# Seven half-block products for the feed-forward up projection of a three-pass fp32 kernel, with weight sums made on VectorE

## The chip, the cores and the metric

The kernel runs on one core of a Trainium2 chip. The metric is the device time of one execution in microseconds (us), as the median over runs. TensorE (PE) multiplies, VectorE (DVE), ScalarE (ACT) and GpSimd (POOL) work on tiles of 128 partitions, and SyncE (SP) issues the loads.

## The reference, cut to what matters

Two blocks of a network run over 512 tokens of width 1024: an attention and a retention layer with memory attention, then a Hyena and gated-linear-attention block. The change touches only the feed-forward part at the very end:

```python
h2 = _rms_norm(x, norm_mlp[l]) * (1.0 + sc2) + sh2          # 512 x 1024
x = x + g2 * (jnp.square(jax.nn.relu(h2 @ w1)) @ w2)         # w1: 1024 x 4096 ("up"), w2: 4096 x 1024 ("down")
return _rms_norm(x, norm_final)
```

## The kernel before

Activations lie transposed: features on the partitions, 512 tokens along the free axis, in tiles of 128 features. A product in fp32 accuracy is made of three passes in the type fp32r. Each operand is split into a high part, rounded by ScalarE, and a low part, the rest; TensorE adds high by high, high by low and low by high into one bank of PSUM.

Weights come in blocks of 512 x 256, stored as 128 x 1024 (four k tiles of 256 columns). One list, PLAN, orders them, and every engine walks it with its own Feed. take() hands out tile u and first makes the splits of all tiles up to u+2. So the split of tile u+2 stands in an engine's instruction stream at the place where that engine takes tile u. For one tile ScalarE copies raw to wh (high), once TensorE has finished tile u-3 (three buffers, NW); GpSimd subtracts to get wl (low). VectorE does that subtraction only for tiles 0 to 72 and tile 164 (DVE_LOW). raw has five buffers, loaded by SyncE as they come free.

In the feed-forward part an up unit is 256 hidden features: two tiles (k halves), each 24 matmuls of 128x512. The unit's features go to banks 0 and 1. ScalarE takes the ReLU out of the bank into a temporary (T1 or T2 in turn), VectorE squares it, ScalarE makes FHI from it and GpSimd FLO; every third FLO is VectorE's. Group g is four up units, 1024 hidden features; a down step (g, n) multiplies the group by the weights for output columns 256n to 256n+255 in two tiles, and VectorE adds the banks, times the gate, onto X. The order is up(0), up(1), down(0), up(2), down(1), up(3), down(2), down(3). All engines execute in program order, so an instruction that waits holds back what is queued behind it.

The rest of the kernel (the two blocks ahead of the feed-forward part) is laid out by the same Feed and isn't touched.

Of the kernel before, what the change touches and what calls it, by code (L numbers as in the profile page):

```python
# [8 lines left out]
ALU = mybir.AluOpType  # L9
# [29 lines left out]

def weight_plan():  # L40
# [3 lines left out]
    def pair(w, k0, k1, cols):  # L44
        for k in range(k0, k1, 4):
            plan.append(("w", w, k, cols))
# [53 lines left out]
    def up(g):  # L100
        for n in range(4):
            pair("up", 0, 8, (1024 * g + 256 * n,))

    def down(g):
        for n in range(4):
            pair("down", 8 * g, 8 * g + 8, (256 * n,))

    up(0)
    for g in range(1, 4):
        up(g)  # L110
        down(g - 1)
    down(3)
# [3 lines left out]
PLAN = weight_plan()  # L116

# [132 lines left out]
def build(nc, a, out, stack):  # L250
# [126 lines left out]
    E = [at("E%d" % j, [128, T], 142 + 2 * j) for j in range(2)]  # L377
    FHI = [at("FHI%d" % g, [128, 8, T], 92 + 32 * g, F32R) for g in range(2)]
    FLO = [at("FLO%d" % g, [128, 8, T], 108 + 32 * g, F32R) for g in range(2)]
# [5 lines left out]
    def P(name, i=0, n=1):  # L385
        o = PAR[name][0] + i
        return par[:, o:o + n]

# [34 lines left out]
    def tensor(pe):  # L423
# [653 lines left out]
        unit_f(("up", 0, 0), (0, 1), *hi_lo("x3"), hooks=[nothing, first_scale, nothing, nothing])  # L1077

        def up(g):
            for n in range(4):  # L1080
                u = 4 * g + n
                if u:
                    unit_f(("up", g, n), (2, 3) if u == 1 else (0, 1), *hi_lo("x4"), by_k=2 if u == 1 else 0)

        def down(g):
            for n in range(4):
                for kh in range(2):
                    u = feed.take()
                    pe.wait_ge(*(done("l", "f", g, k) for k in range(4 * kh, 4 * kh + 4)))
                    features(("down", g, n), FHI[g % 2], FLO[g % 2], range(4 * kh, 4 * kh + 4), kh == 0, kh == 1, (0, 1), u,  # L1090
                             kh=kh)

        up(0)
        for g in range(1, 4):
            up(g)
            down(g - 1)
        down(3)
# [25 lines left out]
    def vector(dve):  # L1123
# [763 lines left out]
        def norm_half(ks, kh):  # L1887

            def low(k):
                dve.wait_ge(done("h", "x4", k))  # L1890
                stt(HL[:, k, :], bank[4 + k % 2], mod[:, 24 + k:25 + k], HH[:, k, :].bitcast(F32), ALU.add,
                    ALU.subtract).then_inc(*by_dve("l", "x4", k))

            for k in ks:
                dve.wait_ge(done("scale rows", "x3"), done("l", "x4", k - 2) if k > 1 else None, *(done("half", ("up", 0, 0), kh, j) for j in range(2)))
                stt(bank[4 + k % 2], X[:, k, :], gx2[:, k:k + 1], bank[7], ALU.mult, ALU.mult).then_inc(*by_dve("x4", k))
                if k > ks[0]:
                    low(k - 1)
            low(ks[-1])

        norm_half(range(0, 4), 0)
        for j in range(2):
            dve.wait_ge(done("unit", ("up", 0, 0), j), done("scale", "x3"))
            tt(E[j][:, :], bank[j], R[:, :], ALU.mult).then_inc(*by_dve("kept", ("up", 0, 0), j))
# [13 lines left out]
        def up(g):  # L1918
            for n in range(4):
                u = 4 * g + n  # L1920
                if u:
                    feed.unit()
                    for j in range(2):
                        k = 2 * n + j
                        t = turn("hidden", g, k)
                        square(g, k, t)
                        if made[0] % 3 == 0:
                            temp_used("hidden", g, k)
                if u == 1:
                    for j in range(2):  # L1930
                        square(g, j, E[j])

        def down(g):
            for n in range(4):
                feed.unit()
                for j in range(2):
                    t = 2 * n + j
                    dve.wait_ge(done("unit", ("down", g, n), j))
                    if g == 3 and t == 7:
                        for h in range(2):  # L1940
                            c = slice(256 * h, 256 * h + 256)
                            stt(X[:, t, c], bank[j][:, c], mod[:, 40 + t:41 + t], X[:, t, c], ALU.mult, ALU.add).then_inc(*by_dve("last tile", h))
                        by_dve.also("kept", ("down", g, n), j)
                        turn("last", "x5")
                        continue
                    stt(X[:, t, :], bank[j], mod[:, 40 + t:41 + t], X[:, t, :], ALU.mult, ALU.add).then_inc(*by_dve("kept", ("down", g, n), j))
                    if g == 3:
                        add_square("x5", t, T, t == 0, t == 6, free=done("sum", "x3"))

        up(0)  # L1950
        for g in range(1, 4):
            up(g)
            down(g - 1)
        down(3)
# [9 lines left out]
    def scalar(act):  # L1964
# [517 lines left out]
        for j in range(2):  # L2482
            act.wait_ge(done("kept", ("up", 0, 0), j), done("shift kept"))
# [7 lines left out]
        def up(g):  # L2491
            for n in range(4):
                u = 4 * g + n
                if u:
                    feed.unit()
                    for j in range(2):
                        k = 2 * n + j
                        t = temp("hidden", g, k)
                        act.wait_ge(done("unit", ("up", g, n), j), temp_free("hidden", g, k))
                        fn(t[:, :], bank[j + 2 * (u == 1)], ACT.Relu).then_inc(*by_act("relu", g, k))  # L2500
                        by_act.also("kept", ("up", g, n), j)
                        high(g, k, t)
                if u == 1:
                    for j in range(2):
                        high(g, j, E[j])

        def down(g):
            for n in range(4):
                feed.unit()
                for j in range(2):  # L2510
                    t, m = 2 * n + j, done("kept", ("down", g, n), j)
                    if g == 3 and t == 7:
                        q = temp("last", "x5")
                        act.wait_ge(temp_free("last", "x5"))
                        for h in range(2):
                            c = slice(256 * h, 256 * h + 256)
                            act.wait_ge(done("last tile", h))
                            fn(q[:, c], X[:, t, c], ACT.Square).then_inc(*by_act("last square half", h))
                    elif g == 3:
                        square("x5", t, X[:, t, :], T, m)  # L2520
                    if g == 3:
                        act.wait_ge(m, done("unit", ("up", 3, 3), 1))
                        fn(XG[:, t, :], X[:, t, :], ACT.Copy, scale=P("gfin", t)).then_inc(*by_act("weighted", t))

        up(0)
        for g in range(1, 4):
            up(g)
            down(g - 1)
        fn(sm[:, 0:1], one, ACT.Sqrt).then_inc(*by_act())
        down(3)  # L2530
# [10 lines left out]
    def gpsimd(pool):  # L2541
        tt = pool.eng.tensor_tensor

        def split(i, u):
            if u not in DVE_LOW:
# [8 lines left out]
                by_pool.also("raw free", i)  # L2554

# [125 lines left out]
        def low(g, k, t):  # L2681
            made[0] += 1
            if made[0] % 3:
# [4 lines left out]
        def up(g):  # L2688
            for n in range(4):
                u = 4 * g + n  # L2690
                if u:
                    feed.unit()
                    for j in range(2):
                        k = 2 * n + j
                        if low(g, k, temp("hidden", g, k)):
                            by_pool.also("temp", turns["hidden", g, k])
                if u == 1:
                    for j in range(2):
                        low(g, j, E[j])

        up(0)
        for g in range(1, 4):
            up(g)
            units(4)
        units(4)
# [190 lines left out]
def layout(x):  # L2896
# [37 lines left out]
    for i, (kind, w, k, cols) in enumerate(plan):  # L2934
        if kind == "w":
# [40 lines left out]
```

## Time and profile before

| | before |
|---|---|
| median of 3 runs | 1625.59 us (1625.49 to 1627.17) |
| the profiled execution | 1626.04 us, of which the span of the trace is 1624.3 us |
| granted TensorE clock, mean | 0.999 |
| busy: TensorE / VectorE / ScalarE / GpSimd | 99% / 51% / 42% / 36% |

The profiled execution lies 0.45 us above the median, and 1.7 us of it lie outside the span. The page gives busy times by engine, the span in 40 slices, and the chain of work that ended last; the trace behind it gives each instruction with its start, its duration, and what ended the idle time before it. The feed-forward part begins with the first up unit at 1265 us.

### The profile page before, as it was taken

What the parts mean: (1) busy time and instruction counts of PE and PEld (TensorE: products, weight loads), DVE (VectorE), ACT (ScalarE), POOL (GpSimd) and SP (SyncE); (2) the same over time, 40 slices, a digit from 0 to 9 for tenths busy, and PEclk for the clock granted to TensorE, in tenths of its full rate; (3) what the DMA queues carried; (4) which work ended last, traced back from release to release, by engine and by line L of the source; (5) the groups of instructions that cost most, each with busy time, mean ns of one, the idle gap of its engine ahead of it and who ended that gap; (6) DMA issues with size and microseconds to landing.
All of it is one profiled execution on the core that took longest, in us unless ns stands there. A gap on an engine that the chain in (4) does not pass through costs nothing.

```text
span 1624.3 us, 20270 instructions
## 1 busy us (share of the span) xinstructions
PE 1607.9 (99%) x8308; PEld 1336.6 (82%) x8308; DVE 829.1 (51%) x1239; ACT 680.8 (42%) x1043; POOL 583.0 (36%) x289
## 2 busy tenths in 40 slices
PE   9999999999999999999999999999999999999998
PEld 6888898889888878888887767789878788888887
DVE  7787867676665364443443646681356621111112
ACT  6533343443432433555455463423435643332323
POOL 1002113221344434334333434353323465555542
PEclk9999999999999999999999999999999999999999
DMA  6453333343355223233223241122112133222221
GB/s 234 153 204 131 125 127 134 116 132 121 133 205 207 104 91 104 93 103 103 94 90 121 78 156 66 52 87 73 53 40 78 65 117 104 91 103 92 98 85 52
DMA packets 53252, 179.16 MB, mean 110 GB/s; under 512 B 6428, under 2 KB 7068, under 8 KB 52776
## 3 DMA queue, kind: packets, MB, share of 16 engines
q1 hardware_dynamic: 53160, 177.88, 31.5%
q8 instruction: 65, 1.06, 0.3%
q14 instruction: 27, 0.22, 0.0%
HBM read 172.58 MB, written 2.12 MB: 108 GB/s over the span
## 4 chain that ended last, share of the span: by engine, by line
PE 92%; DVE 5%; ACT 1%; issue 1%; DMA 0%; SPq 0%; POOL 0%; DVEq 0%; ACTq 0%; POOLq 0%
PE banks L427 90%; PE banks L430 2%; DVE ACC L1182 1%; DVE wl L1146 1%; ACT T L1969 0%; DMA maskf<-cst_dram 0%; DVE ada L1130 0%; DVE X L1130 0%; ACT wh L1972 0%; ACT Sc L1969 0%; DVE ML L1130 0%; DVE T L1912 0%; ACT L1969 0%; DVE Sc L1130 0%; DVE E L1912 0%
## 5 line engine op out<-in xcount | busy, mean ns | idle before, releaser
L2553 POOL TENSOR_TENSOR wl<-raw,wh 128x1024 fp32r<-128x1024 f32 x171 | 424.2, 2485 | 525.3 <-ACT wh L1972 525.3
L427 PE MATMUL banks<-HH,wh 128*128 128x512 f32 (+1 forms) x1040 | 413.2, 397 | 2.6 <-ACT T L1969 0.9
L427 PE MATMUL banks<-HL,wh 128*128 128x512 f32 (+1 forms) x1040 | 402.3, 390 | 0.3 <-DVE HL L1130 0.3
L1972 ACT ACTIVATE wh<-raw 128x1024 fp32r<-128x1024 f32 x246 | 257.0, 1052 | 296.9 <-PE banks L427 289.0
L427 PE MATMUL banks<-HH,wl 128*128 128x512 f32 x1032 | 282.6, 390 | 0.0
L427 PEld LDWEIGHTS banks<-HH,wh 128*128 128x128 f32 (+1 forms) x1040 | 194.9, 187 | 50.0 <-issue 5.5
L427 PEld LDWEIGHTS banks<-HL,wh 128*128 128x128 f32 (+1 forms) x1040 | 194.7, 187 | 42.0 <-issue 1.4
L427 PEld LDWEIGHTS banks<-HH,wl 128*128 128x128 f32 x1032 | 193.4, 188 | 41.5 <-issue 1.0
L427 PE MATMUL banks<-wh,HH 128*128 128x256 f32 x448 | 128.5, 287 | 0.0
L427 PE MATMUL banks<-wl,HH 128*128 128x256 f32 x448 | 126.7, 283 | 0.0
L427 PE MATMUL banks<-wh,HL 128*128 128x256 f32 x448 | 126.6, 283 | 0.0
L1146 DVE TENSOR_TENSOR wl<-raw,wh 128x1024 fp32r<-128x1024 f32 x74 | 89.5, 1231 | 28.3 <-ACT wh L1972 28.3
L427 PE MATMUL banks<-OH,wh 128*128 128x512 f32 x256 | 103.1, 403 | 0.3 <-issue 0.3
L1130 DVE SCALAR_TENSOR_TENSOR X<-banks,mod,X 128x512 f32<-128x512 f32 (+1 forms) x41 | 30.1, 736 | 142.3 <-PE banks L427 142.3
L427 PE MATMUL banks<-OL,wh 128*128 128x512 f32 x256 | 99.8, 390 | 0.0
L427 PE MATMUL banks<-FHI,wh 128*128 128x512 f32 x256 | 99.6, 389 | 0.0
L427 PE MATMUL banks<-FLO,wh 128*128 128x512 f32 x256 | 99.6, 389 | 0.0
L2562 POOL TENSOR_TENSOR OL<-T,OH 128x512 fp32r<-128x512 f32 x21 | 28.3, 1349 | 197.4 <-ACT OH L1972 197.4
L1912 DVE TENSOR_TENSOR T<-T 128x512 f32<-128x512 f32 x30 | 28.3, 942 | 113.9 <-ACT T L1969 113.8
L427 PEld LDWEIGHTS banks<-wh,HL 128*128 128x128 f32 x448 | 85.7, 191 | 0.5 <-issue 0.2
L427 PEld LDWEIGHTS banks<-wh,HH 128*128 128x128 f32 x448 | 85.7, 191 | 0.5 <-issue 0.2
L427 PEld LDWEIGHTS banks<-wl,HH 128*128 128x128 f32 x448 | 85.7, 191 | 0.0
(354 smaller groups left out, 2627.5 us busy)
## 6 DMA issues: line engine op xcount, KB each, us to landing
raw<-wst_dram SPq DMA_DIRECT2D x294, 512.0 KB, 3.2
X<-xT_dram SPq DMA_DIRECT2D x8, 512.0 KB, 6.6
CB<-sums_dram SPq DMA_DIRECT2D x12, 256.0 KB, 3.1
D<-dec_dram SPq DMA_DIRECT2D x12, 256.0 KB, 2.8
out_dram<-XT SPq DMA_DIRECT2D x8, 256.0 KB
QS<-QX SPq DMA_DIRECT2D x24, 64.0 KB, 2.6
KSw<-KX SPq DMA_DIRECT2D x24, 64.0 KB, 2.0
MX<-memT_dram SPq DMA_DIRECT2D x2, 512.0 KB, 8.7
```

What stands on the lines that cost most here:

```text
L427: return pe.eng.matmul(dst, w, x, start=start, stop=stop, skip_group_check=True)
L430: return pe.eng.transpose(dst, x, ident[:, :])
L1130: return eng.scalar_tensor_tensor(out=dst, in0=x, scalar=s, in1=y, op0=op0, op1=op1)
L1146: tt(wl[:, q, :], raw[:, i % NRAW, :], wh[:, q, :].bitcast(F32), ALU.subtract).then_inc(*by_dve("low", u))
L1182: i = tt(acc[:, 0:n], acc[:, 0:n], q[:, 0:n], ALU.add)
L1912: tt(t[:, :], t[:, :], t[:, :], ALU.mult).then_inc(*by_dve("f", g, k))
L1972: return eng.activation(dst, src, ACT.Copy)
L2553: tt(wl[:, q, :], raw[:, i % NRAW, :], wh[:, q, :].bitcast(F32), ALU.subtract).then_inc(*by_pool("low", u))
L2562: tt(OL[:, tile, :], t[:, :], OH[:, tile, :].bitcast(F32), ALU.subtract).then_inc(*by_pool("l", "o", l, tile))
```

## The change

Up units 4 to 15 are computed by Winograd's form of Strassen's scheme. A tile of 512 x 256 weights and the matching 512 x 512 of activations are cut into 2 x 2 half blocks (two k tiles by 128 output features; two k tiles by 256 tokens). Seven products replace eight; four of them take sums of weight blocks, four take sums of activation blocks. The products of one unit go to halves of banks 2 to 5 and are put together by VectorE. Moving operands become 256 wide. For each such tile (kind "s") ScalarE copies the raw tile to banks 6 and 7, VectorE makes four sums from that copy and the raw tile, ScalarE and GpSimd make their high and low parts. VectorE also makes wl of these tiles. The group becomes two up units (512 hidden features), a down step becomes one tile, and the order becomes: up(0), up(1), then for g from 1 to 7 and h in 0, 1: up(2g+h), down(g-1, 2h), down(g-1, 2h+1); at the end down(7, 0..3). Nothing changes ahead of the second up unit.

```diff
+FF = [("up", 0), ("up", 1)]
+for _g in range(1, 8):
+    for _h in range(2):
+        FF += [("up", 2 * _g + _h), ("down", _g - 1, 2 * _h), ("down", _g - 1, 2 * _h + 1)]
+FF += [("down", 7, _n) for _n in range(4)]
+SEVEN = 4
+NS = 3
# TensorE
+        def seven(u):
+            for kh in range(2):
+                w = feed.take()
...
+                def product(b, c, a, x):
+                    o, s0 = bank[b][:, 256 * c:256 * c + 256], kh == 0 and c == 0
+                    for q in range(2):
+                        mm(o, a[0][:, q, :], x[0][:, q, :], s0 and q == 0, False)
+                        mm(o, a[0][:, q, :], x[1][:, q, :], False, False)
+                    for q in range(2):
+                        i = mm(o, a[1][:, q, :], x[0][:, q, :], False, kh == 1 and q == 1)
+                    return i
+                pe.wait_ge(done("high", w), done("low", w), done("x sums", kh), *free[2])
+                product(2, 0, of_w(1, 0), of_x(1, 0))
+                product(2, 1, of_w(0, 0), of_x(0, 0)).then_inc(*by_pe("seven", u, kh, 0))
+                pe.wait_ge(done("sums high", w), done("sums low", w), *free[3])
+                product(3, 0, of_w(1, 1), of_t(3))
+                product(3, 1, of_s(2), of_t(1)).then_inc(*by_pe("seven", u, kh, 1))
+                pe.wait_ge(*free[4])
+                product(4, 0, of_s(1), of_t(0))
+                product(4, 1, of_s(0), of_t(2)).then_inc(*by_pe("seven", u, kh, 2))
+                pe.wait_ge(*free[5])
+                product(5, 0, of_s(3), of_x(1, 1)).then_inc(*by_pe("seven", u, kh, 3))
...
+        def down(g, n):
+            u = feed.take()
+            pe.wait_ge(*(done("l", "f", g, k) for k in range(4)))
+            features(("down", g, n), FHI[g % 2], FLO[g % 2], range(4), True, True, (0, 1), u)
# VectorE
         def split(i, u):
-            if u in DVE_LOW:
+            if PLAN[i][0] == "s":
...
+                dve.wait_ge(done("copied", u), done("sums low", S_TILES[v - 2]) if v > 1 else done("l", "f", 0, 1))
+                tt(s[:, 0:2, :, :], c[:, 0, :, :, :].rearrange("p q i c -> p i q c"), w[:, :, :, 1, :],
+                   ALU.subtract).then_inc(*by_dve())
+                dve.wait_ge(by_dve.last())
+                tt(s[:, 2, :, :], c[:, 1, :, 1, :], s[:, 0, :, :], ALU.add).then_inc(*by_dve())
+                dve.wait_ge(by_dve.last())
+                tt(s[:, 3, :, :], c[:, 1, :, 0, :], s[:, 2, :, :], ALU.subtract).then_inc(*by_dve("summed", i))
+                dve.wait_ge(done("high", u))
+                tt(wl[:, q, :], psum[:, 6:8, :].rearrange("p b c -> p (b c)"), wh[:, q, :].bitcast(F32),
+                   ALU.subtract).then_inc(*by_dve("low", u))
+                by_dve.also("raw free", i)
+            elif u in DVE_LOW:
...
+        def x_sums(kh):
+            x = XW[:, 4 * kh:4 * kh + 4, :].rearrange("p (j q) (h c) -> p j q h c", q=2, c=256)
...
+            tt(XS[0][:, 0, :, :], b12, b11, ALU.subtract).then_inc(*by_dve())
+            stt(XS[1][:, 0, :, :], b22, -1.0, b12, ALU.mult, ALU.subtract).then_inc(*by_dve())
+            dve.wait_ge(by_dve.last())
+            tt(XS[0][:, 1, :, :], b22, XS[0][:, 0, :, :], ALU.add).then_inc(*by_dve("x summed", kh, 0))
+            dve.wait_ge(by_dve.last())
+            tt(XS[1][:, 1, :, :], b21, XS[0][:, 1, :, :], ALU.subtract).then_inc(*by_dve("x summed", kh, 1))
+        def x_sums_low(kh):
+            for n in range(2):
+                dve.wait_ge(done("x sums high", kh, n), done("x summed", kh, 1))
+                tt(XSL[:, kh, 2 * n:2 * n + 2, :, :], XS[n][:, :, :, :], XSH[:, kh, 2 * n:2 * n + 2, :, :].bitcast(F32),
+                   ALU.subtract).then_inc(*by_dve("x sums", kh))
+        def seven(u):
+            g, n = u // 2, 2 * (u % 2)
+            kept = done("kept", ("up", u - 1), 0) if u > SEVEN else None
+            dve.wait_ge(done("seven", u, 1, 1), done("first product", u), kept)
+            tt(PS[:, 1, :], bank[3][:, 256:512], PS[:, 0, :], ALU.add).then_inc(*by_dve())
+            dve.wait_ge(done("seven", u, 1, 2), by_dve.last())
+            tt(PS[:, 2:4, :], psum[:, 4, :].rearrange("p (a c) -> p a c", a=2), PS[:, 1:2, :].to_broadcast([128, 2, 256]),
+               ALU.add).then_inc(*by_dve())
+            t = turn("hidden", g, n + 1)
+            dve.wait_ge(by_dve.last(), temp_free("hidden", g, n + 1))
+            tt(t[:, :].rearrange("p (a c) -> p a c", a=2), psum[:, 3:5, 0:256], PS[:, 3:4, :].to_broadcast([128, 2, 256]),
+               ALU.add).then_inc(*by_dve("kept", ("up", u), 1))
+            hidden(g, n + 1, t)
+            t = turn("hidden", g, n)
+            dve.wait_ge(done("seven", u, 1, 3), temp_free("hidden", g, n))
+            tt(t[:, :].rearrange("p (a c) -> p a c", a=2), psum[:, 2:6:3, 0:256], PS[:, 0:3:2, :],
+               ALU.add).then_inc(*by_dve("kept", ("up", u), 0))
+            hidden(g, n, t)
+        def hidden(g, k, t):
+            dve.wait_ge(by_dve.last())
+            stt(t[:, :], t[:, :], 0.0, t[:, :], ALU.max, ALU.mult).then_inc(*by_dve("f", g, k))
...
+        def down(g, n):
+            feed.take()
+            for j in range(2):
...
+                stt(X[:, t, :], bank[j], mod[:, 40 + t:41 + t], X[:, t, :], ALU.mult, ALU.add).then_inc(*by_dve("kept", ("down", g, n), j))
...
+            if (g, n) == (0, 0):
+                x_sums_low(0)
+            if (g, n) == (0, 1):
+                x_sums(1)
# in VectorE's up(u): after u == 2 x_sums(0), after u == 3 x_sums_low(1)
# ScalarE
         def split(i, u):
+            if PLAN[i][0] == "s":
+                v = S_AT[u]
+                act.wait_ge(done("low", S_TILES[v - 1]) if v else done("l", "x4", 7))
+                copy(psum[:, 6:8, :].rearrange("p b c -> p (b c)"), raw[:, i % NRAW, :]).then_inc(*by_act("copied", u))
             copy(wh[:, u % NW, :], raw[:, i % NRAW, :]).then_inc(*by_act("high", u))
+            if PLAN[i][0] == "s":
+                act.wait_ge(done("summed", i), done("w free", S_TILES[v - NS]) if v >= NS else None)
+                copy(SH_[:, v % NS, :], WS[:, v % 2, :]).then_inc(*by_act("sums high", u))
...
+            if u >= SEVEN:
+                act.wait_ge(done("seven", u, 1, 0), done("kept", ("up", u - 1), 0) if u > SEVEN else done("x sums", 1))
+                copy(PS[:, 0, :], bank[2][:, 256:512]).then_inc(*by_act("first product", u))
+                for k in (2 * (u % 2) + 1, 2 * (u % 2)):
+                    high(g, k, temp("hidden", g, k))
+                return
# GpSimd
+            if PLAN[i][0] == "s":
+                v = S_AT[u]
+                pool.wait_ge(done("sums high", u))
+                tt(SL_[:, v % NS, :], WS[:, v % 2, :], SH_[:, v % NS, :].bitcast(F32), ALU.subtract).then_inc(*by_pool("sums low", u))
...
+        def x_whole(k):
+            pool.wait_ge(done("h", "x4", k), done("l", "x4", k))
+            tt(XW[:, k, :], HH[:, k, :].bitcast(F32), HL[:, k, :].bitcast(F32), ALU.add).then_inc(*by_pool("x whole", k))
+        def up(u):
+            feed.unit()
...
+            if u in (1, 2):
+                for k in range(4 * u - 4, 4 * u):
+                    x_whole(k)
```

## Rows read from the trace of the kernel before

**Rows 1.** The page: busy time by engine, then the chain that ended last.
```profile
PE 1607.9 (99%) x8308; PEld 1336.6 (82%) x8308; DVE 829.1 (51%) x1239; ACT 680.8 (42%) x1043; POOL 583.0 (36%) x289
PE 92%; DVE 5%; ACT 1%; issue 1%; DMA 0%; SPq 0%; POOL 0%; DVEq 0%; ACTq 0%; POOLq 0%
```
**Rows 2.** Busy time in a stretch: us, PE, PEld, DVE, ACT, POOL (instructions), clock, DMA.
```profile
1439.30:1482.00 42.70, 42.70 (x190) 35.36 (x189) 6.64 (x9) 9.60 (x10) 20.13 (x9) 1.00 0.26 95
```
**Rows 3.** Timeline of TensorE, 512 wide: start, duration, operation, count.
```profile
1402.83 0.39 PE L427 MATMUL banks<-HL,wh 128*128 128x512 f32 x1
1403.05 1.07 PE L427 MATMUL banks<-HH,wl 128*128 128x512 f32 x4
1403.96 0.39 PE L427 MATMUL banks<-HH,wh 128*128 128x512 f32 x1
```
**Rows 4.** Timeline of TensorE, weights from wh and wl, 256 wide.
```profile
31.73 0.28 PE L427 MATMUL banks<-ML,wh 128*128 128x256 f32 x1
32.57 0.64 PE L427 MATMUL banks<-MH,wl 128*128 128x256 f32 x4
33.05 0.28 PE L427 MATMUL banks<-MH,wh 128*128 128x256 f32 x1
```
**Rows 5.** Timeline across engines, a down step and the split beside it.
```profile
1461.34 1.06 ACT L1972 ACTIVATE wh<-raw 128x1024 fp32r<-128x1024 f32 x1 [4.38 <-PE banks L427]
1466.78 1.06 ACT L1972 ACTIVATE wh<-raw 128x1024 fp32r<-128x1024 f32 x1 [4.38 <-PE banks L427]
1450.40 0.75 DVE L1130 SCALAR_TENSOR_TENSOR X<-banks,mod,X 128x512 f32<-128x512 f32 x1 [1.97 <-PE banks L427]
```
**Rows 6.** Groups by form, VectorE: count, busy us, mean ns.
```profile
L1904 DVE TENSOR_TENSOR E<-banks,R 128x512 f32<-128x512 f32 x2 | 1.3, 680 | 0.0
L1368 DVE TENSOR_TENSOR PL<-banks,PH 128x256 fp32r<-128x256 f32 x12 | 5.0, 413 | 0.0
L1130 DVE SCALAR_TENSOR_TENSOR T<-X,gfx,R 128x512 f32<-128x512 f32 x8 | 5.9, 751 | 0.2
```
**Rows 7.** One line of VectorE: duration ns min/median/max.
```profile
L1146 DVE TENSOR_TENSOR wl<-raw,wh x74: 1208/1217/1714, 6.3 to 1074.2; 128x1024 fp32r<-128x1024 f32 x74
```
**Rows 8.** Groups by form, ScalarE and GpSimd.
```profile
L1972 ACT ACTIVATE FHI<-T 128x512 fp32r<-128x512 f32 x30 | 19.0, 633 | 30.3 <-DVE T L1912 30.3
L1969 ACT ACTIVATE banks<-R 128x512 f32<-128x512 f32 x1 | 0.6, 602 | 0.0
L2553 POOL TENSOR_TENSOR wl<-raw,wh 128x1024 fp32r<-128x1024 f32 x64 | 154.2, 2412 | 132.7 <-ACT wh L1972 132.7
```
**Rows 9.** Timeline, the opening of the feed-forward part: VectorE and GpSimd.
```profile
1284.57 5.20 POOL L2553 TENSOR_TENSOR wl<-raw,wh 128x1024 fp32r<-128x1024 f32 x2 [9.97 <-ACT wh L1972]
1286.11 1.40 DVE L1912 TENSOR_TENSOR T<-T 128x512 f32<-128x512 f32 x1 [1.78 <-ACT T L1969]
1288.70 1.62 DVE L1912 TENSOR_TENSOR T<-T 128x512 f32<-128x512 f32 x1 [1.19 <-ACT T L1969]
1289.73 3.44 POOL L2685 TENSOR_TENSOR FLO<-T,FHI 128x512 fp32r<-128x512 f32 x2
1295.06 1.30 POOL L2685 TENSOR_TENSOR FLO<-E,FHI 128x512 fp32r<-128x512 f32 x1 [1.89 <-ACT FHI L1972]
1296.31 5.21 POOL L2553 TENSOR_TENSOR wl<-raw,wh 128x1024 fp32r<-128x1024 f32 x2
```
**Rows 10.** Timeline of TensorE at the start of the fourth up unit.
```profile
1297.51 0.47 PE L427 MATMUL banks<-HH,wh 128*128 128x512 f32 x1 [0.94 <-ACT T L1969]
```
**Rows 11.** Timeline, hand-overs VectorE to ScalarE to GpSimd.
```profile
1407.51 0.69 DVE L1912 TENSOR_TENSOR T<-T 128x512 f32<-128x512 f32 x1 [1.93 <-ACT T L1969]
1408.23 0.63 ACT L1972 ACTIVATE FHI<-T 128x512 fp32r<-128x512 f32 x1 [0.76 <-DVE T L1912]
```
**Rows 12.** Waits of TensorE on others, longest in total: us, times, longest.
```profile
PE banks L427 <- DVE wl L1146: 2.3, 4, 1.0
PE banks L427 <- DVE Z L1263: 1.2, 1, 1.2
```

More of the change, by code:

```diff
@@ L1075, in first_scale @@
             free[6] = (done("sum kept", "x3"),)
[L1077 to L1091, printed above, removed]
@@ L1933, in down @@
-        def down(g):
-            for n in range(4):
-                feed.unit()
-                for j in range(2):
[L1937 to L1948, printed above, removed]
@@ new lines, in down @@
+        def down(g, n):
+            feed.take()
+            for j in range(2):
+                t = 2 * n + j
+                dve.wait_ge(done("unit", ("down", g, n), j), done("kept", ("down", g - 1, n), j) if g else None)
+                if g == 7 and t == 7:
+                    for h in range(2):
+                        c = slice(256 * h, 256 * h + 256)
+                        stt(X[:, t, c], bank[j][:, c], mod[:, 40 + t:41 + t], X[:, t, c], ALU.mult, ALU.add).then_inc(*by_dve("last tile", h))
+                    by_dve.also("kept", ("down", g, n), j)
+                    turn("last", "x5")
+                    continue
+                stt(X[:, t, :], bank[j], mod[:, 40 + t:41 + t], X[:, t, :], ALU.mult, ALU.add).then_inc(*by_dve("kept", ("down", g, n), j))
+                if g == 7:
+                    add_square("x5", t, T, t == 0, t == 6, free=done("sum", "x3"))
+            if (g, n) == (0, 0):
+                x_sums_low(0)
+            if (g, n) == (0, 1):
+                x_sums(1)
@@ L1955, in vector @@
+        for step in FF[1:]:
+            (up if step[0] == "up" else down)(*step[1:])
         dve.wait_ge(done("root"))
@@ L2489, in high @@
             copy(FHI[g % 2][:, k, :], t[:, :]).then_inc(*by_act("h", "f", g, k))
[L2491 to L2505, printed above, removed]
@@ L2507, in down @@
-        def down(g):
-            for n in range(4):
-                feed.unit()
-                for j in range(2):
[L2511 to L2530, printed above, removed]
+        def x_sums_high(kh):
+            for n in range(2):
+                act.wait_ge(done("x summed", kh, n))
+                copy(XSH[:, kh, 2 * n:2 * n + 2, :, :], XS[n][:, :, :, :]).then_inc(*by_act("x sums high", kh, n))
+        def up(u):
+            feed.unit()
+            g = u // 2
+            if u >= SEVEN:
+                act.wait_ge(done("seven", u, 1, 0), done("kept", ("up", u - 1), 0) if u > SEVEN else done("x sums", 1))
+                copy(PS[:, 0, :], bank[2][:, 256:512]).then_inc(*by_act("first product", u))
+                for k in (2 * (u % 2) + 1, 2 * (u % 2)):
+                    high(g, k, temp("hidden", g, k))
+                return
+            for j in range(2):
+                k = 2 * (u % 2) + j
+                t = temp("hidden", g, k)
+                act.wait_ge(done("unit", ("up", u), j), temp_free("hidden", g, k))
+                fn(t[:, :], bank[j + 2 * (u == 1)], ACT.Relu).then_inc(*by_act("relu", g, k))
+                by_act.also("kept", ("up", u), j)
+                high(g, k, t)
+            if u == 1:
+                for j in range(2):
+                    high(g, j, E[j])
+            if u == 2:
+                x_sums_high(0)
@@ new lines, in down @@
+        def down(g, n):
+            if (g, n) == (7, 0):
+                fn(sm[:, 0:1], one, ACT.Sqrt).then_inc(*by_act())
+            feed.take()
+            for j in range(2):
+                t, m = 2 * n + j, done("kept", ("down", g, n), j)
+                if g == 7 and t == 7:
+                    q = temp("last", "x5")
+                    act.wait_ge(temp_free("last", "x5"))
+                    for h in range(2):
+                        c = slice(256 * h, 256 * h + 256)
+                        act.wait_ge(done("last tile", h))
+                        fn(q[:, c], X[:, t, c], ACT.Square).then_inc(*by_act("last square half", h))
+                elif g == 7:
+                    square("x5", t, X[:, t, :], T, m)
+                if g == 7:
+                    act.wait_ge(m, done("seven", 15, 1, 3))
+                    fn(XG[:, t, :], X[:, t, :], ACT.Copy, scale=P("gfin", t)).then_inc(*by_act("weighted", t))
+            if (g, n) == (0, 1):
+                x_sums_high(1)
@@ L2531, in scalar @@
+        for step in FF[1:]:
+            (up if step[0] == "up" else down)(*step[1:])
         act.wait_ge(done("sum col", "x5"))
@@ L2544, in split @@
         def split(i, u):
-            if u not in DVE_LOW:
+            if u not in DVE_LOW and u not in S_AT:
                 q = u % NW
@@ L2686, in low, with up @@
                 return True
[L2688 to L2705, printed above, removed]
+        def x_whole(k):
+            pool.wait_ge(done("h", "x4", k), done("l", "x4", k))
+            tt(XW[:, k, :], HH[:, k, :].bitcast(F32), HL[:, k, :].bitcast(F32), ALU.add).then_inc(*by_pool("x whole", k))
+        def up(u):
+            feed.unit()
+            g = u // 2
+            for k in (1, 0) if u >= SEVEN else (0, 1):
+                k += 2 * (u % 2)
+                if low(g, k, temp("hidden", g, k)):
+                    by_pool.also("temp", turns["hidden", g, k])
+            if u == 1:
+                for j in range(2):
+                    low(g, j, E[j])
+            if u in (1, 2):
+                for k in range(4 * u - 4, 4 * u):
+                    x_whole(k)
+        for step in FF[1:]:
+            if step[0] == "up":
+                up(step[1])
+            else:
+                feed.take()
     def sync(sp):
```

113 lines of the change are left out of this document (67 added, 46 removed).

## The prediction

> **What bounds the kernel now.** I read the page first. TensorE is busy for 99% of the span and is 92% of the chain that ended last, at the full clock [rows 1]. Then the busy times of one stretch in the feed-forward part: TensorE is busy for all 42.7 us of it, VectorE for 6.6, ScalarE for 9.6, GpSimd for 20.1 [rows 2]. The others have room on average. So there are two ways to move the time: fewer TensorE cycles, or a place where TensorE waits. The longest wait now is 1.2 us [rows 12].
>
> What the pace of TensorE is comes from starts, not from durations, since matmuls overlap. Four matmuls of 512 columns take 1403.05 to 1403.96, which is 0.227 each, and the one ahead of them 0.22 [rows 3]. A tile has 24 of them: 5.44 us. The starts of the copy to wh, each released by TensorE, lie 5.44 apart too [rows 5]. Matmuls of 256 columns with weights from wh or wl take 31.73 to 33.05 for 11 starts, 0.12 each, the same for high and low weights [rows 4]. Two narrow ones cost 0.24 against 0.227 for one wide.
>
> **TensorE's work.** An up unit of two tiles takes 48 x 0.227 = 10.88 us. In sevens it takes 7 products x 6 matmuls x 2 tiles = 84 x 0.12 = 10.08. So one eighth fewer cycles becomes 0.80 us per unit, and 12 x 0.80 = **9.6 us less**. The other tiles keep their matmuls. The price of the narrow form is from rows of the same form, so I take no range for it beyond 0.3 us per unit for its waits.
>
> **The wait that is added in each step.** The order per unit is now: tiles A0 and A1 (the unit), D0 and D1 (two down steps, one tile each), then B0 and B1, the next unit. A split stands where tile u-2 is taken, so the split of B0 stands in down(D0), ahead of the two additions onto X on VectorE, and in ScalarE's stream behind the copies to FHI of the unit before. Until now VectorE had no split in this part. D1 uses banks 0 and 1 like D0, so TensorE can't begin D1 until VectorE has added bank 0 of D0. Let A1 start at 0. D0 ends at 5.04 + 5.44 = 10.48, and that is when bank 0 is wanted.
>
> When is it free? A product is over 0.72 us after the one before it, and is seen 0.28 - 0.12 = 0.16 later [rows 4] plus 0.03 to 0.04 for a hand-over [rows 11], so product n at 0.72n + 0.20. The sixth at 4.52. Then on VectorE:
> two additions with an operand in PSUM at 0.68 each [rows 6], the second dependent, to 5.9;
> the square of the first half, a scalar_tensor_tensor of 512, 0.75 [rows 6], to 6.7;
> the addition for the second half (0.68) and its square (0.75), to 8.1. The seventh product (5.24) isn't waited for.
> ScalarE: FHI of that half, 0.63 [rows 8], to 8.75; the copy of raw to PSUM. No row shows such a copy of 1024; a 1024 wide copy SBUF to SBUF takes 1.06 [rows 5] and a write of 512 to PSUM 0.60 against 0.63 for 512 to SBUF [rows 8], so 1.0 to 1.06; to about 9.75.
> VectorE: the sums, 0.68 for the 512 wide one and 0.41 for each 256 wide one [rows 6], dependent on each other, to 11.3; wl, 1.22 by the same subtraction in SBUF [rows 7], to 12.45; the addition onto X, 0.75 [rows 5], to **13.15**.
> I let neighbours that don't depend on each other overlap by 0.07, as two do in 1.3 us for 2 x 0.68 [rows 6].
>
> TensorE waits 13.18 - 10.48 = **2.7 us**. Bank 1 is free 0.7 later and wanted 2.7 later, so it adds nothing. The split of B1 is late by as much but has D1 and B0 as cover: its low sums are made at about 19 and wanted after 23. GpSimd's part for B0 (2.41 [rows 8]) ends near 14.8, wanted at 18.6. So the pattern repeats from A1 of the next unit with the same wait. It comes once behind each of units 4 to 14 (behind unit 15 there is no such split, and the chain ends at 8.9): 11 x 2.7 = **29.7 us more**. Bounds: 2.2 if all small gaps vanish and PSUM writes are quick, 4.0 by the lock below. It costs nothing only if the chain were 2.7 us shorter, more than a quarter of its 8.6.
>
> **The port between VectorE and GpSimd.** A subtraction of GpSimd runs 1284.57 to about 1287; a 512 wide multiply of VectorE with its input in SBUF, issued at 1286.11, takes 1.40 in place of 0.69, the next one 1.62 until the second subtraction is over [rows 9, 11]. The additions onto X keep 0.75 beside a busy GpSimd [rows 5]. So operations with an operand in PSUM go through, others take turns with GpSimd. The Trainium skill, SBUF — State Buffer, section "Who interferes with whom", says the same of VectorE with two inputs in SBUF, and that the one that starts first has the ports for the whole instruction; by that rule the squares are exposed as well, scalar_tensor_tensor or not. In my chain the last square starts 0.6 us behind the end of the first and GpSimd's FLO, behind ScalarE's 0.63, 0.12 us later. If the order flips, the chain gets 1.3 us longer.
>
> **The opening.** Sums of activations are new work between up(1) and up(4). GpSimd is nearly full there: its last FLO of up(1) ends at 1296.36, and two subtractions follow at once [rows 9]. Four additions x_whole (1.29 each, as FLO) come between, to 1301.5, then wl of down(0,0), 2.4 and a turn of VectorE, to 1304.6. TensorE starts that step at 1297.5 [rows 10] and wants wl after 8 matmuls, at 1299.3: 5.3 us. VectorE then does x_sums(0), four operations with two inputs in SBUF, in turn with GpSimd's 2.4, 1.3, 1.3, from 1304.5 to 1313.4, ahead of the addition onto X of down(0,0), done at 1314.1 and wanted at 1308.2: 5.9. x_sums_low(0), two of 1.22 behind GpSimd's next two, puts the X of down(0,1) to 1321.5, wanted at 1319.5: 2.0. Behind up(3), x_sums_low(1) stands ahead of the first split: 3.3. Less the 0.4 lost there now, **16 us more**. Bounds: 7 if the turns cost nothing (4.6 of GpSimd's own and 2), 25 if they double.
>
> **Off the path.** 32 more additions onto X (0.75 each), 12 copies of a first product and 24 x 2 more copies on ScalarE lie beside TensorE, apart from those in the chain above. Loads keep their number and lead.
>
> **The sum**, against the profiled execution: 1626.0 - 9.6 + 29.7 + 16 = 1662.1. The median lies 0.45 below that execution, so about 1662. The best end of the three terms gives 1626 - 9.6 + 24 + 7 = 1647, the worst 1626 - 9.6 + 44 + 25 = 1685.
>
> **The rivals.**
> 1. Faster: bank 0 is added in time, because VectorE's chain between the sixth product and X is under 6 us. Then only the opening's own 7 us or less stand against 9.6: 1616 to 1623. It decides from a wait under 0.8 us less what the opening costs. For it speaks the room of VectorE on average [rows 2]; against it the order of the queue, which no spare time mends. 1 in 10.
> 2. The lock goes to GpSimd at the last square: 4.0 us for each wait, 11 x 1.3 = 14 more, 1676. For it the margin of 0.12; 18%.
> 3. The opening costs only its lower bound: 1653. 15%.
>
> **Numbers.** The forecast 50%; rivals as above; 2% for something between that ends within 0.2% of before, which is about what a measurement of this kernel can tell from no change. The range 1646 to 1684 takes in the forecast with its bounds and rivals 2 and 3, and leaves out 1 and 4. Faster by over 0.2%: 0.10; within: 0.03; slower: 0.87.
>
> **What the changed profile would show.** Starts of 256 wide matmuls 0.12 apart, 10.1 us per unit. An idle TensorE of about 2.7 us ahead of the second down step behind each unit from 4 to 14, ended by VectorE's addition onto X, and none behind unit 15. VectorE's order there: square, sums, wl, X without much idle. Two gaps of over 4 us between 1297 and 1320, the first ended by GpSimd's wl. GpSimd no longer near 2.4 us per tile of an up unit. I am wrong if X of D0 comes ahead of its bank's next use, or if the sums come without waiting for ScalarE's FHI.

## The result and the profile after

The changed kernel takes 1664.82 us (median of 4, 1664.29 to 1667.28) against 1625.73 us of the kernel before beside it. The ratio is 1.0242, with a 95% interval from 1.0224 to 1.0259: 39 us slower. The forecast was 1662, within 1646 to 1684.

The page of the changed kernel: span, busy time by engine, and the chain that ended last.

```profile
span 1663.2 us, 21488 instructions
PE 1607.4 (97%) x8740; PEld 1352.1 (81%) x8740; DVE 959.1 (58%) x1419; ACT 722.9 (43%) x1083; POOL 615.0 (37%) x305
PE 83%; DVE 10%; ACT 3%; issue 2%; DMA 0%; POOL 0%; SPq 0%; DVEq 0%; ACTq 0%; POOLq 0%
```

Beside [rows 1]: TensorE's share of the chain falls from 92% to 83%, and VectorE's doubles to 10%. TensorE is busy for as long as before, 1607 us, though it has one eighth fewer cycles in 12 units. Part of that time it ran at half speed, as shown below.

Waits of TensorE in the changed kernel: us in total, times, longest. The first two are new beside [rows 12].

```profile
PE banks L445 <- DVE X L1188: 33.9, 13, 5.6
PE banks L445 <- POOL wl L2691: 5.4, 1, 5.4
PE banks L445 <- DVE wl L1219: 2.3, 4, 1.0
```

The timeline of TensorE shows where they lie: the two large waits of the opening, then one per unit, of which three stand here. All of them but the first end with an addition onto X.

```profile
1304.17 2.07 PE L445 MATMUL banks<-FHI,wl 128*128 128x512 f32 x4 [5.42 <-POOL wl L2691]
1311.55 0.50 PE L445 MATMUL banks<-FHI,wh 128*128 128x512 f32 x1 [0.97 <-DVE X L1188]
1339.51 0.79 PE L445 MATMUL banks<-FHI,wh 128*128 128x512 f32 x1 [5.56 <-DVE X L1188]
...
1388.97 0.47 PE L445 MATMUL banks<-FHI,wh 128*128 128x512 f32 x1 [2.48 <-DVE X L1188]
1412.72 0.47 PE L445 MATMUL banks<-FHI,wh 128*128 128x512 f32 x1 [2.48 <-DVE X L1188]
1436.46 0.47 PE L445 MATMUL banks<-FHI,wh 128*128 128x512 f32 x1 [2.48 <-DVE X L1188]
```

There are 11 of the last kind, each 2.48 or 2.49 us, with starts 23.75 us apart (1388.97 to 1412.72). The kernel before spent 4 tiles x 5.44 = 21.76 us on the same work [rows 5]. The idle time is counted from the modelled end of the last matmul, 0.16 behind its slot, so the true delay is about 2.65.

The chain behind the wait that ends at 1412.72, on VectorE and then on ScalarE. The unit's second tile starts at 1399.57.

```profile
1404.09 0.69 DVE L2017 TENSOR_TENSOR PS<-banks,PS 128x512 f32<-128x512 f32 x1 [1.01 <-PE banks L445]
1404.81 0.69 DVE L2021 TENSOR_TENSOR T<-banks,PS 128x512 f32<-128x512 f32 x1
1405.54 0.69 DVE L1188 SCALAR_TENSOR_TENSOR T<-T 128x512 f32<-128x512 f32 x1
1406.15 0.68 DVE L2026 TENSOR_TENSOR T<-banks,PS 128x512 f32<-128x512 f32 x1
1406.87 0.69 DVE L1188 SCALAR_TENSOR_TENSOR T<-T 128x512 f32<-128x512 f32 x1
1409.17 0.69 DVE L1206 TENSOR_TENSOR WS<-banks,raw 128x512 f32<-128x512 f32 x1 [1.61 <-ACT banks L2093]
1409.90 0.42 DVE L1209 TENSOR_TENSOR WS<-banks,WS 128x256 f32<-128x256 f32 x1
1410.36 0.42 DVE L1211 TENSOR_TENSOR WS<-banks,WS 128x256 f32<-128x256 f32 x1
1410.70 1.21 DVE L1213 TENSOR_TENSOR wl<-banks,wh 128x1024 fp32r<-128x1024 f32 x1
1411.83 1.40 DVE L1188 SCALAR_TENSOR_TENSOR X<-banks,mod,X 128x512 f32<-128x512 f32 x2
...
1407.59 0.63 ACT L2093 ACTIVATE FHI<-T 128x512 fp32r<-128x512 f32 x1 [0.69 <-DVE T L1188]
1408.13 1.01 ACT L2093 ACTIVATE banks<-raw 128x1024 f32<-128x1024 f32 x1
```

The one idle time of VectorE in it, 1.61 us, is for ScalarE's FHI and copy. The addition onto X comes last, though its bank had been complete since about 1407.5.

Busy time in short stretches behind four waits (columns as in [rows 2]; the clock is the number behind POOL's): the waits were 5.42, 5.56, 2.48 and 2.48 us.

```profile
1304.00:1308.00 4.00, 3.83 (x9) 3.06 (x10) 3.97 (x3) 0.00 (x0) 4.00 (x3) 0.50 0.44 139
1339.50:1343.00 3.50, 3.49 (x8) 2.81 (x9) 3.19 (x5) 2.48 (x3) 1.92 (x2) 0.50 0.43 150
1460.21:1464.00 3.79, 3.79 (x11) 3.03 (x12) 3.09 (x5) 2.37 (x3) 2.20 (x2) 0.61 0.43 138
1412.72:1416.00 3.28, 3.28 (x14) 2.70 (x15) 3.21 (x6) 2.38 (x3) 1.71 (x2) 1.00 0.49 160
```

Behind both long waits TensorE ran at a granted clock of 0.50, that is 1.2 in place of 2.4 GHz. Behind one of the 11 short ones (that at 1460.21) it was 0.61 over 3.8 us; behind that at 1412.72 it was 1.00, and the steps of the others are 23.7 to 23.8 us long like its own. The costs: the step from 1296.69 to the idle time at 1310.58 took 13.9 us, of which 5.44 are its tile, 5.42 its wait and 0.32 the ends of two matmuls behind their slots, so 2.7 for the clock; the period behind 1339.51 took 25.72 against 23.75, so 2.0 (the same work); the one behind 1460.21 25.13, so 1.4. Together 6.1 us.

### The profile page after: what moved, and what is told of

It is laid out like the page before. It is cut to its first block, busy times and chain, and to the rows that moved or that the text cites. A ratio compares the mean times of both kernels' runs of the same rounds, so it can differ in the third digit from the quotient of the medians.

```text
span 1663.2 us, 21488 instructions
## 1 busy us (share of the span) xinstructions
PE 1607.4 (97%) x8740; PEld 1352.1 (81%) x8740; DVE 959.1 (58%) x1419; ACT 722.9 (43%) x1083; POOL 615.0 (37%) x305
## 4 chain that ended last, share of the span: by engine, by line
PE 83%; DVE 10%; ACT 3%; issue 2%; DMA 0%; POOL 0%; SPq 0%; DVEq 0%; ACTq 0%; POOLq 0%
PE banks L445 81%; PE banks L448 2%; DVE ACC L1255 1%; DVE X L1188 1%; DVE wl L1213 1%; DVE wl L1219 1%; ACT banks L2093 1%; DVE T L1188 1%; DVE WS L1206 1%; ACT T L2090 0%; ACT wh L2093 0%; DVE PS L2017 0%; DVE T L2021 0%; DVE T L2026 0%; DMA maskf<-cst_dram 0%
## 5 line engine op out<-in xcount | busy, mean ns | idle before, releaser
L2691 POOL TENSOR_TENSOR wl<-raw,wh 128x1024 fp32r<-128x1024 f32 x147 | 368.4, 2512 | 481.1 <-ACT wh L2093 481.1
L445 PE MATMUL banks<-HH,wh 128*128 128x512 f32 (+2 forms) x944 | 363.3, 387 | 1.8 <-ACT PH L2093 0.8
L445 PE MATMUL banks<-HL,wh 128*128 128x512 f32 (+2 forms) x944 | 352.8, 379 | 0.3 <-DVE HL L1188 0.3
L445 PE MATMUL banks<-HH,wl 128*128 128x512 f32 (+1 forms) x936 | 250.5, 379 | 0.0
L445 PEld LDWEIGHTS banks<-HH,wh 128*128 128x128 f32 (+1 forms) x944 | 177.2, 188 | 41.6 <-issue 6.0
L445 PEld LDWEIGHTS banks<-HL,wh 128*128 128x128 f32 (+1 forms) x944 | 177.0, 188 | 35.3 <-issue 1.4
L445 PEld LDWEIGHTS banks<-HH,wl 128*128 128x128 f32 x936 | 172.3, 188 | 33.9 <-issue 1.0
L445 PE MATMUL banks<-FHI,wh 128*128 128x512 f32 x256 | 103.9, 406 | 34.9 <-DVE X L1188 33.9
L445 PEld LDWEIGHTS banks<-FHI,wh 128*128 128x128 f32 x256 | 49.7, 194 | 50.2 <-ACT SH L2093 31.7
L2729 POOL TENSOR_TENSOR CM<-CB,mask 128x512 f32<-128x512 f32 x12 | 34.5, 2875 | 122.4 <-DMA CB<-sums_dram 122.4
```

The lines of the kernel that those rows point to most:

```text
L445: return pe.eng.matmul(dst, w, x, start=start, stop=stop, skip_group_check=True)
L2729: tt(CM[:, :].rearrange("p (i m) -> p i m", i=4), CB[:, :].rearrange("p (i m) -> p i m", i=4), mask[:, :].rearrange("p (i m) -> p i m", i= ...
```

## The experiments

Ratios and medians stand beside runs of the kernel before on the same chip, 1625.4 to 1625.9 us.

**The new order alone, and with the activations' sums.** `order_only` has no unit in sevens and no sums of activations; the groups and down steps are those of the changed kernel.

```diff
-SEVEN = 4
+SEVEN = 16
-            if u == 2:
-                x_sums(0)
-            if u == 3:
-                x_sums_low(1)
...
-            if u in (1, 2):
-                for k in range(4 * u - 4, 4 * u):
-                    x_whole(k)
```

> The new order alone: groups of two up units, down steps of one tile, all up units with eight products in wide matmuls, no sums of activations. My theory puts the whole loss on the sums and on the place of the new splits, so this one should take 1625 to 1627 us, with no wait of TensorE over 1.2 us. The rival, that the smaller groups and the 32 more additions onto X cost time themselves, would show 1630 or more.

Measured: 1627.09 us, ratio 1.0010 (1.0000 to 1.0019). So the order costs 1.6 us, by the interval something from 0 to 3.1; that is at the upper end of what was expected, and below the rival's 1630. The trace shows one new wait of 1.0 us, for an addition onto X ahead of the second down step.

`order_sums` differs from the changed kernel by `SEVEN = 16`, and by one wait of ScalarE at the very end that named the last product in sevens: the sums of activations are made, and no product uses them.

> The new order with the sums of activations in the opening, no unit in sevens. In the changed kernel the opening shows TensorE waiting 5.4 us for GpSimd's wl and 1.0 us for an addition onto X, and about 3 us at the lower clock behind the first. If GpSimd's four additions ahead of that wl are the cause, both stay here: 1626 + 10 = 1636 us. The 5.6 us behind the fourth up unit should shrink to under 3, since no split of a seven tile follows. If the splits of the seven tiles were behind all of it, 1626.

Measured: 1639.67 us, ratio 1.0088 (1.0073 to 1.0103), 12.6 more than the order alone. TensorE's timeline and GpSimd's in this kernel:

```profile
1304.37 2.07 PE L445 MATMUL banks<-FHI,wl 128*128 128x512 f32 x4 [5.42 <-POOL wl L2691]
1337.05 0.79 PE L445 MATMUL banks<-FHI,wh 128*128 128x512 f32 x1 [2.93 <-DVE X L1188]
...
1295.70 5.87 POOL L2832 TENSOR_TENSOR XW<-HH,HL 128x512 f32<-128x512 f32 x4
1301.53 5.56 POOL L2691 TENSOR_TENSOR wl<-raw,wh 128x1024 fp32r<-128x1024 f32 x2
```

GpSimd's four additions stand ahead of the wl for which TensorE waits 5.42 us, with no seven in the kernel, and in `order_only`, without them, that wait is gone. That cause is shown. I was 3.7 us low: behind the third wait (2.93 us) the clock was 0.60 over four microseconds too, and I had not priced that.

**The addition onto X ahead of the split.** `add_first` changes VectorE's stream in a down step.

```diff
-            feed.take()
             for j in range(2):
+                if j:
+                    feed.take()
                 t = 2 * n + j
```

> The changed kernel with one line moved: in a down step VectorE adds the first bank onto X before it takes the next tile's split, not after. My theory: the wait of 2.5 us behind each of the 11 units goes (11 x 2.65 with the drain, and 2.7 of slower matmuls behind those waits), and of the 5.6 us behind the fourth unit about half and its slow clock: 1665 - 29 - 3 - 5 = 1628 us. If the wait came from VectorE's total work or from ScalarE, it would stay and the time be above 1650.

Measured: 1630.30 us, ratio 1.0029 (1.0018 to 1.0041): 34.5 us are back, from one moved line, and 2.3 us above what was expected. All waits of TensorE over 0.25 us behind 1290 us in this kernel:

```profile
1296.83 0.47 PE L445 MATMUL banks<-FHI,wh 128*128 128x512 f32 x1 [0.97 <-ACT T L2091]
1304.30 2.08 PE L445 MATMUL banks<-FHI,wl 128*128 128x512 f32 x4 [5.39 <-POOL wl L2692]
1311.68 0.50 PE L445 MATMUL banks<-FHI,wh 128*128 128x512 f32 x1 [1.73 <-DVE X L1188]
1336.98 0.50 PE L445 MATMUL banks<-FHI,wh 128*128 128x512 f32 x1 [2.92 <-DVE X L1188]
1340.28 0.50 PE L445 MATMUL banks<-FHI,wh 128*128 128x512 f32 x1 [0.29 <-DVE X L1188]
```

The 11 waits are gone with the same operations on every engine, so they came from the place of the split in the queue. Of those of the opening the first stays. The second grew from 0.97 to 1.73 us, and the one behind the fourth unit fell from 5.56 to 2.92, about half as expected.

**An eighth product, ahead of the chain's start and behind it.** Both kernels add one product per unit into the free half of bank 5. `eighth_open` has it at the end of the first tile, `eighth_covered` in the second tile behind the sixth product.

```diff
# eighth_open
                 product(5, 0, of_s(3), of_x(1, 1)).then_inc(*by_pe("seven", u, kh, 3))
+                if kh == 0:
+                    product(5, 1, of_s(3), of_x(1, 1)).then_inc(*by_pe())
# eighth_covered
+                if kh == 1:
+                    product(5, 1, of_s(3), of_x(1, 1)).then_inc(*by_pe())
                 product(5, 0, of_s(3), of_x(1, 1)).then_inc(*by_pe("seven", u, kh, 3))
```

> The changed kernel with one product more per unit (6 matmuls of 256 columns into a half bank that nobody reads), at the end of the unit's first tile. It lies ahead of the point from which the chain to the addition onto X starts, so my theory has it cost all of its 6 x 0.12 = 0.72 us, 12 times: 1665 + 8.6 = 1673.5 us, with the same wait of 2.5 us.

> The same extra product, in the unit's second tile behind the sixth product, from which the chain starts. By my theory it only fills the wait: TensorE waits 1.8 in place of 2.5 us in 11 units and the time stays at 1665 to 1666 us. If the wait hung on the end of TensorE's unit or on the drained down tile, it would cost 0.72 x 12 as the other one and give 1673.

Measured: 1678.02 us (ratio 1.0322, 1.0306 to 1.0338) and 1663.98 us (1.0237, 1.0219 to 1.0256). The same matmuls cost 13 us in one place and nothing in the other. The wait of a steady step, first in `eighth_open`, then in `eighth_covered`:

```profile
1415.62 0.47 PE L445 MATMUL banks<-FHI,wh 128*128 128x512 f32 x1 [2.48 <-DVE X L1190]
```
```profile
1412.21 0.47 PE L445 MATMUL banks<-FHI,wh 128*128 128x512 f32 x1 [1.76 <-DVE X L1190]
```

2.48 - 1.76 = 0.72 us is the product, taken out of the wait. So the chain starts in the unit's second tile, at the sixth product at the latest, and not at the unit's end. In `eighth_open` the expected 8.6 us became 13.2. Most steps are 24.43 us, the 0.69 more that was expected, but three are 26.1, 1.65 longer, where the changed kernel has one such step. That makes 3.3 of the 4.6 missing; another 0.9 lies in the step behind the wait at the fourth unit, which took 27.3 us where 25.7 and the product make 26.4. `eighth_covered` has none of them in its steady steps (23.7 each), which is why it comes out below the changed kernel.

**The sums without the copy in PSUM.**

```diff
-                w, c = blocks(raw[:, i % NRAW, :]), blocks(psum[:, 6:8, :].rearrange("p b c -> p (b c)"))
+                w = c = blocks(raw[:, i % NRAW, :])
...
-                copy(psum[:, 6:8, :].rearrange("p b c -> p (b c)"), raw[:, i % NRAW, :]).then_inc(*by_act("copied", u))
```

> The changed kernel without ScalarE's copy of the tile to PSUM: VectorE makes the sums and wl from the raw tile in SBUF. That takes 1.0 us of ScalarE out of the chain. Without contention the wait falls from 2.5 to 1.5 and the time to about 1653 us. By the turns that VectorE and GpSimd take, the sums now wait for GpSimd's two FLO subtractions of the unit, which end at about the time at which the copy ended: wait 2.5 to 3.3, time 1663 to 1674 us.

Measured: 1681.69 us, ratio 1.0345 (1.0328 to 1.0363). A steady step in this kernel, VectorE and GpSimd:

```profile
1435.06 1.78 DVE L1206 TENSOR_TENSOR WS<-raw 128x512 f32<-128x512 f32 x1
1436.88 1.39 DVE L1209 TENSOR_TENSOR WS<-raw,WS 128x256 f32<-128x256 f32 x1
1438.31 0.42 DVE L1211 TENSOR_TENSOR WS<-raw,WS 128x256 f32<-128x256 f32 x1
...
1434.56 3.43 POOL L2825 TENSOR_TENSOR FLO<-T,FHI 128x512 fp32r<-128x512 f32 x2 [3.62 <-ACT FHI L2093]
...
1440.68 0.47 PE L445 MATMUL banks<-FHI,wh 128*128 128x512 f32 x1 [2.86 <-DVE X L1188]
```

The sums take 1.78 and 1.39 us in place of 0.69 and 0.42, as long as GpSimd's two FLO run beside them, and 0.42 once these are over at 1437.99. The wait of TensorE grows from 2.48 to 2.86 although ScalarE has one operation less in the chain. So the copy in PSUM is worth having: with it the sums at 1409.17 and 1413.14 took 0.69 and 0.68 us beside a busy GpSimd. The wait came as expected (2.5 to 3.3), the time did not: 11 x 0.38 = 4 us of 17. Of the ten steps between its waits one took 24.10 us and nine 25.5 to 25.7; the clock fell in them (0.61 over the 3.8 us behind the wait that ends at 1415.17). Ten such stretches (the nine steps, and the one behind the last wait) against one in the changed kernel make 9 x 1.5 = 13 us, about the rest. I had not priced it.

**Sums of activations with cover, and sevens from unit 6.** These kernels keep `add_first` and spread the opening's new work.

```diff
-SEVEN = 4
+SEVEN = 6
 # GpSimd: two x_whole per down step of group 0, behind the step's split
+                if step[1:] in ((0, 0), (0, 1), (0, 2), (0, 3)):
+                    for k in range(2 * step[2], 2 * step[2] + 2):
+                        x_whole(k)
 # VectorE, late_sums, ahead of the squares of up(u)
+            if u == 3:
+                x_sums(0)
+            if u == 4:
+                x_sums_low(0)
+                x_sums(1)
+            if u == 5:
+                x_sums_low(1)
```

> As the moved line, and the sums of activations spread over up units 3 to 5 (GpSimd's additions two per down step, behind its subtraction), with sevens from unit 6 on. 10 units x 0.8 us saved and nothing lost in the opening: 1626 - 8 = 1618 us. If something else costs in the opening or in each step, it stays at or above 1626.

Measured: 1622.16 us, ratio 0.9980 (0.9970 to 0.9990): a little faster than before, 4 us above what was expected. TensorE waited 1.41 and 1.10 us for ReLUs behind units 3 and 4, and 1.00 in the first down steps, which the new order brings.

> As late_sums, but each half of the low parts of the activations' sums in a down step of its own, behind the additions onto X, and ScalarE's high parts behind its ReLUs. In late_sums TensorE waited 1.4 and 1.1 us for a ReLU behind up units 3 and 4. If those sums held up the squares and with them the ReLUs, both waits go: 1622.2 - 2.5 = 1619.7 us. The wait of 1.0 us ahead of the second down step, which the new order alone has too, stays.

Measured: 1622.66 us, ratio 0.9982 (0.9973 to 0.9992). A miss. Both waits are gone and one of 2.42 us for a ReLU is there: x_sums(1) now waited for GpSimd's last x_whole until 1338.3, and the squares stood behind it.

> As spread_sums, but the second half of the activations' sums in the fifth up unit after the first, and its low parts in the two down steps behind it. In spread_sums VectorE waited until 1338.3 for GpSimd's last x_whole, and TensorE then 2.4 us for a ReLU. One unit later GpSimd is done long before, so that wait goes: 1622.7 - 2.4 = 1620.3 us. If the wait only moves along with the sums, it stays at 1622 or more.

Measured: 1621.90 us, ratio 0.9978 (0.9969 to 0.9987). That is 1.6 above what was expected, and what the rival says: the wait moved again, now 1.74 us for the last low part of the sums in the first unit in sevens.

```diff
# sums_ahead against even_sums, VectorE's down step
                 if j:
+                    if (g, n) == (1, 3):
+                        x_sums_low(1, 1)
                     feed.take()
```

> As even_sums, with the last low part of the activations' sums ahead of the split in its down step instead of behind the second addition onto X. In even_sums TensorE waited 1.7 us for exactly that subtraction in the first unit in sevens. It goes, the splits behind it have cover: 1621.9 - 1.7 = 1620.2 us. If it is only traded for a later split, the time stays at 1622.

Measured: **1620.16 us** (median of 5, 1620.11 to 1620.54), ratio 0.9965 (0.9951 to 0.9979). The wait of 1.74 us is gone from its trace, and one of 0.35 us for GpSimd's low part of a split stands near its place. It is the fastest kernel of the study, 5.8 us below the kernel before beside it and 44.7 below the changed one, though its interval overlaps that of `even_sums`. Its page:

```profile
PE 1600.7 (99%) x8668; PEld 1347.4 (83%) x8668; DVE 944.5 (58%) x1397; ACT 715.4 (44%) x1077; POOL 606.4 (37%) x303
```

**How much a unit in sevens saves.**

> As even_sums with sevens from up unit 12 on instead of 6, so 4 units in place of 10. If the saving is 0.8 us per unit and nothing else comes with a unit in sevens, this one is 6 x 0.8 = 4.8 us slower than even_sums. If the steps still lose something small (a late bank, a first matmul that starts slower), the difference is smaller.

Measured: 1623.56 us, 1.7 above even_sums instead of 4.8. Of the missing 3.1, 1.9 are the two waits that even_sums has at its first unit in sevens (1.74) and just ahead of it (0.16) and this one has not. The other 1.2 are no more than these intervals leave open (0.0009 of 1625 us is 1.5). In the traces of even_sums and add_first the steady steps are 21.0 us apart, against 21.76 before, so a unit saves 0.75 us in practice. By that 10 x 0.75 = 7.5 us are saved, and sums_ahead keeps 5.8 of them; the order's 1.6 us is about the rest.

## Why the prediction was right, point by point

- **TensorE's work, -9.6 us.** Right. Narrow matmuls start 0.12 apart, and the period fits 10.08 per unit; without waits it comes to 0.75 saved per unit, of 0.80.
- **The chain behind a unit, +29.7.** Right in each link, to 0.2 us. From the start of the second tile: sixth product seen at 4.52 (forecast 4.52), second square over at 7.99 (8.1), copy in PSUM at 9.57 (9.75), sums at 11.2 (11.3), wl at 12.3 (12.45), next down step at 13.15 (13.18). 11 x 2.65 = 29.2, and 1.3 for slower first matmuls. The order of the queue, one moved line, is its cause (`add_first`), and its start the sixth product (`eighth_covered`).
- **The opening, +16.** Right in sum, wrong in parts. What is left of the 38.9 us of span once the other terms are taken (9.6 saved, 29.2, 1.3, and 1.4 at 1460.21) is 16.6. The part ahead of the feed-forward took 0.8 us less in this trace, so by the feed-forward part alone it is 17.4: three waits with the ends of matmuls before them 12.4, the slow clock behind two of them 4.7. But the four waits forecast as 5.3, 5.9, 2.0 and 3.3 were 5.42, 0.97, none and 5.56. The first is right, by the cause I gave. The lines for the others:

```profile
1301.84 2.82 DVE L1997 TENSOR_TENSOR XS<-XW 128x512 f32<-128x512 f32 x1
1304.59 2.85 DVE L1188 SCALAR_TENSOR_TENSOR XS<-XW 128x512 f32<-128x512 f32 x1
1312.07 4.47 DVE L2007 TENSOR_TENSOR XSL<-XS,XSH 128x1024 fp32r<-128x1024 f32 x2
1331.63 4.51 DVE L2007 TENSOR_TENSOR XSL<-XS,XSH 128x1024 fp32r<-128x1024 f32 x2
```

The second was 4.9 us shorter for two reasons. x_sums(0) took 9.0 us, as forecast (8.9, though the turns that the forecast names add up to 7.8), but it started at 1301.84, beside GpSimd's wl, and not at 1304.5 behind it: counted from the start of the down step, the addition onto X came 1.8 us sooner. And TensorE, at half speed, wanted the bank 3.0 us later. For the third, x_sums_low(0) took 4.5 us where the forecast had about 6. For the last, x_sums_low(1) took 4.5 us, with GpSimd's FLO beside it, where the forecast's 3.3 fits two operations of 1.22 without turns. So the step that failed is the working of when VectorE and GpSimd take turns, and for how long. The clock wasn't in the sum at all: it made the second wait shorter and cost 4.7 us itself, and that the total came out is luck. The 0.4 taken off for a wait of the kernel before had no ground either: it is 0.94 us before [rows 10] and 1.00 after.
- **The clock, rival 4.** It was given 5% and left out of the sum. It isn't a case of its own but a term beside the waits: 6.1 us here. The Trainium skill (TensorE: Matmul & The Clock Gate, section "Part 1: The HAM clock gate") says that the clock falls when TensorE has stood idle. The rows above agree in direction, with 0.50 behind waits of 5.4 and 5.6 us.
- **The port, rival 2.** It did not come. The last square starts at 1406.87 and GpSimd's FLO at 1406.97, 0.10 later where 0.12 was forecast. The Trainium skill, SBUF — State Buffer, section "Who interferes with whom", has a VectorE instruction with two inputs in SBUF contend with a GpSimd instruction that reads SBUF. `raw_sums` agrees (1.78 us in place of 0.69), and so does the line at 1304.59 above, a scalar_tensor_tensor: 2.85 us.
- **Faster, rival 1.** It did not come: from the sixth product to X the chain took 8.5 us, where the rival needs under 6. With the queue mended it is 1630, because the opening still costs more than the 9.6 us; the kernels that spread the opening's work fell below the kernel before.
- **Smaller slips.** The range was said to take in the bounds, but its top, 1684, lies under the worst end, 1685. Two gaps of over 4 us between 1297 and 1320 were to show, and only one did; the other stands at 1339. GpSimd was to leave its 2.4 us per tile of an up unit, and still spends them, on the low part of the weight sums (2.396 us on average, 24 times).

## What to carry to other kernels

A split, load or conversion made two tiles ahead is hidden only if the engine that makes it has nothing urgent behind it in its queue. Before giving such work to an engine with spare time, write down that engine's stream at this point and ask who waits for the next entry: here an addition of 0.75 us that frees a bank stood behind 2.7 us of work that itself waited 1.6 us for ScalarE. Busy shares (VectorE 51% before, 58% after) say nothing on that.

## What the runs showed of the hardware

- TensorE's clock behind waits of one length, by the ten steady steps between its waits, in one trace of each kernel: none was slowed in `eighth_covered` (waits of 1.76 us), one in the changed kernel and three in `eighth_open` (2.48 us), nine in `raw_sums` (2.86 us). Each slow step was 1.4 to 1.7 us longer than its neighbours. The length of the wait alone doesn't settle it: behind 2.93 us in `order_sums` the clock was 0.60 over four microseconds, behind 2.92 us at the same place in `add_first` it was 1.00. The four executions of `raw_sums` differ with it too, from 1678.48 us at a mean clock of 0.988 to 1684.77 at 0.984. What else sets it I can't say from these runs.
- ScalarE wrote a 128x1024 copy to PSUM in 1.02 us against 1.05 for the one to SBUF. VectorE's subtraction with an operand in PSUM took 1.215 us for 1024 columns, as in SBUF; GpSimd ran beside none of the 24, so they don't show how it fares there. The 512 wide sum with an operand in PSUM did have GpSimd beside it (at 1409.17, for one) and took 0.68 to 0.69 us all 24 times.
